# Pooling products in pairs between the gate projections, and five modulation units loaded into the work area

## The reference, cut to what matters

```python
h, gate_res = ada_modulate(x, c, norm_g, ada_w, ada_b)     # norm, scale and shift: silu(c) @ ada_w + ada_b
a, u, v, gate = split(h @ in_w)                            # four slices of 1024, 1024, 1024 and 2048 columns
ya = pool_mixer(a, pool_w, pool_scale)                     # windowed means, then 4 products of 256 x 256
yb = spatial_gating(u, v, sgu_norm_g, sgu_w, sgu_b)
y = concatenate([ya, yb]) * silu(gate)
x = x + gate_res * (y @ out_w)                             # 2048 x 1024
```

## Time and profile before

| What | us |
|---|---|
| median of three runs | 939.27 |
| the profiled execution, its own time | 939.58 |
| its span, first to last instruction | 937.8 |
| PE busy | 916.1 |
| DVE busy | 646.7 |
| ACT busy | 508.9 |

### The profile page before, as it was taken

How to read it: one execution, slowest core, us unless ns; L and a number is a source line. 1 busy time by engine, 2 the same in 40 slices (tenths; PEclk the granted TensorE clock), 3 DMA queues, 4 the chain that set the end, 5 groups by cost and what they waited for, 6 DMA issues and landing times.

```text
span 937.8 us, 19578 instructions
## 1 busy us (share of the span) xinstructions
PE 916.1 (98%) x8685; PEld 891.4 (95%) x8685; DVE 646.7 (69%) x754; ACT 508.9 (54%) x604; POOL 2.1 (0%) x14
## 2 busy tenths in 40 slices
PE   7999999999999999999999999999999999999998
PEld 6899999999999999999899999899889999999997
DVE  2897988785577467767689886557777665465565
ACT  3445445445554567963475654376646653455445
POOL 0000000000000000000000000000000000000000
PEclk9999999999999999999999999999999999999998
DMA  9999547974667544467444452234444556556521
GB/s 338 364 363 355 181 139 229 299 228 144 191 211 229 178 135 136 135 206 243 142 136 151 137 166 92 87 95 135 148 137 155 178 182 225 180 181 211 170 91 46
DMA packets 153440, 172.31 MB, mean 184 GB/s; under 512 B 4000, under 2 KB 137692, under 8 KB 153228
## 3 DMA queue, kind: packets, MB, share of 16 engines
q1 hardware_dynamic: 151696, 167.43, 55.2%
q10 hardware_dynamic: 1660, 3.63, 1.1%
HBM read 170.00 MB, written 1.05 MB: 182 GB/s over the span
## 4 chain that ended last, share of the span: by engine, by line
PE 79%; DVE 10%; ACT 5%; issue 3%; DMA 2%; ACTq 1%; DVEq 0%
PE pj L2695 64%; DVE w_lo L1502 2%; DMA work<-in_x_dram 1%; PE pj L2651 1%; ACT w_hi L1002 1%; PE pj L2653 1%; PE pj L2652 1%; PE pj L2480 1%; PE m_all L2387 1%; PE m_all L2370 1%; ACTq L965 1%; DMA rows<-in_ple_post_norm_dram 1%; PE m_all L2119 1%; DVE work L1935 0%; DVE work L2091 0%
## 5 line engine op out<-in xcount | busy, mean ns | idle before, releaser
L1502 DVE TENSOR_TENSOR w_lo<-raw,w_hi 128x2048 fp32r<-128x2048 f32 (+1 forms) x126 | 285.1, 2268 | 133.3 <-ACT w_hi L1002 132.6
L2695 PE MATMUL pj<-h_hi,w_hi 128*128 128x256 f32 (+1 forms) x1176 | 333.4, 284 | 2.3 <-issue 1.0
L2695 PE MATMUL pj<-h_lo,w_hi 128*128 128x256 f32 (+1 forms) x1176 | 328.3, 279 | 0.0
L2695 PE MATMUL pj<-h_hi,w_lo 128*128 128x256 f32 (+1 forms) x1176 | 328.1, 279 | 0.0
L1002 ACT ACTIVATE w_hi<-raw 128x2048 fp32r<-128x2048 f32 (+1 forms) x126 | 237.8, 1891 | 52.1 <-PE pj L2695 25.8
L2695 PEld LDWEIGHTS pj<-h_hi,w_hi 128*128 128x128 f32 (+1 forms) x1176 | 219.9, 187 | 6.0 <-issue 3.8
L2695 PEld LDWEIGHTS pj<-h_lo,w_hi 128*128 128x128 f32 (+1 forms) x1176 | 220.0, 187 | 0.4
L2695 PEld LDWEIGHTS pj<-h_hi,w_lo 128*128 128x128 f32 (+1 forms) x1176 | 219.9, 187 | 0.2
L2695 PE MATMUL pj<-y_lo,w_hi 128*128 128x256 f32 x624 | 174.2, 279 | 0.0
L2695 PE MATMUL pj<-y_hi,w_hi 128*128 128x256 f32 x592 | 165.7, 280 | 2.2 <-issue 2.2
L2695 PE MATMUL pj<-y_hi,w_lo 128*128 128x256 f32 x592 | 165.1, 279 | 0.0
(11 more groups left out here) (417 smaller groups left out, 1129.2 us busy)
## 6 DMA issues: line engine op xcount, KB each, us to landing
raw<-in_odd_in_w_dram SPq DMA_DIRECT2D x28, 1024.0 KB, 5.2
raw<-in_w_in_dram SPq DMA_DIRECT2D x23, 1024.0 KB, 5.3
raw<-in_ada_w_dram SPq DMA_DIRECT2D x22, 1024.0 KB, 7.4
raw<-in_w_ff_in_dram SPq DMA_DIRECT2D x16, 1024.0 KB, 5.4
raw<-in_w_ff_out_dram SPq DMA_DIRECT2D x16, 1024.0 KB, 5.1
raw<-in_even_in_w_dram SPq DMA_DIRECT2D x13, 1024.0 KB, 5.2
raw<-in_even_out_w_dram SPq DMA_DIRECT2D x8, 1024.0 KB, 6.1
raw<-in_odd_out_w_dram SPq DMA_DIRECT2D x8, 1024.0 KB, 5.1
```

The lines of the kernel that those rows point to most:

```text
L1502: V.tensor_tensor(lo[:, 0:n], raw_of(u)[:, 0:n], hi[:, 0:n].bitcast(F32), ALU.subtract).then_inc(done, 1)
L2695: m = nc.tensor.matmul(to, a_, b_, start=(s == 0 and q == 0 and (fb == 0 or not together)), stop=(s == len(steps_) - 1 and q == 2), skip_g ...
```

## The change

Four things change. The pooling jobs 0 and 1 stay before `ega` 0, but 2 and 3 now stand between `ega` 0 and `ega` 1. The modulation units that stand behind `ega` jobs stand behind 0 and 2, where it was 1 and 3. Five modulation units (15 to 19, now with the unit numbers 33, 36, 40, 43 and 46) no longer use the ring: they land in the work area, at places 0 and 35 in turn, once what lies there has been used. SP waits for that before it issues them.

```diff
-EARLY = {3: 8, 4: 16, 5: 24, 9: 116, 11: 124, 15: 116, 17: 124, 19: 116, 21: 124}
-REUSED = {9: 3, 11: 4, 15: 9, 17: 11, 19: 15, 21: 17}
+EARLY = {3: 8, 4: 16, 5: 24, 9: 116, 11: 124, 15: 116, 17: 124, 19: 116, 21: 124, 33: 0, 36: 35, 40: 0, 43: 35, 46: 0}
+REUSED = {9: 3, 11: 4, 15: 9, 17: 11, 19: 15, 21: 17, 33: 19, 36: 21, 40: 33, 43: 36, 46: 40}
-ADA_BEHIND = {"ev": (1, 2, 3), "ea": (0, 1, 2, 3), "ega": (1, 3)}
+ADA_BEHIND = {"ev": (1, 2, 3), "ea": (0, 1, 2, 3), "ega": (0, 2)}
...
-    def even(name, kind, w, c0, layout_="F"):
+    def even(name, kind, w, c0, layout_="F", before={}):
 
         for i in range(4):
+            for g in before.get(i, ()):
+                pool(g)
             job(name, kind, i, layout_, ...)
...
-    for g in range(4):
+
+    def pool(g):
         job("pool", "pool", g, "F", [pool_u], 2, 8 + 2 * g, lambda xc: ("p_lo", 1), k0=2 * g)
         jobs["pool", g]["late"] = True
-    even("ega", "gate", even_w, 3072)
+
+    even("ega", "gate", even_w, 3072, before={0: (0, 1), 1: (2, 3)})
...
                     if units[REUSED[u]]["ada"] is None:
                         split_done(sp, units[REUSED[u]])
+                    else:
+                        sp.wait_ge(S("ada_acc"), ADA_DVE.index(units[REUSED[u]]["ada"][2]) + 1)
+                if u == 33:
+                    sp.wait_ge(S("sgu_z"), 4)
+                if u == 36:
+                    sp.wait_ge(S("y_f"), 4)
```

## The result

The changed kernel takes 941.36 us (median of 9 runs, 940.16 to 942.57), the kernel before 938.19 us on the same chip (9 runs, 937.61 to 939.63). The ratio is 1.003, 95% interval 1.002 to 1.004: slower by about 3.2 us. The forecast was 941.8 us on a base of 939.27; as a difference it was +2.5 us. That 941.8 lies only 0.4 us from the measured time is partly luck: the base was 1.1 us higher than in this timing, and the difference 0.7 us too small.

A forecast was written before the change was run, and what follows sets the result against it. PE was taken as the bound, busy 916.1 of 937.8 us. Terms 0.53 + 2.1 + 0.3 less 0.33 gave +2.5 us, 942.1 on the profiled 939.58; less 0.3 to the median, 941.8 us, range 939.2 to 943.6.

The forecast's parts named there:

- Before `ega` 0: PE, with two pooling jobs less in front, waits for DVE's split: gap 1.55 us instead of 1.02, loss 0.53.
- Before `ega` 3: PE waits for DVE's late split of `ega` 3, which had been 2 us early: `ega` 3 starts 2.1 us late.
- Both named causes: Before `ega` 3: ACT's wait for the pooling jobs, and unit 16 and pooling copies, 4.7 us of DVE, before the split.
- Before `eo` 1: PE waits for DVE's split of `eo` 1: gap 1.4 us instead of 1.06, start 2.85 us later than before.
- signs named in advance: Expected in the changed kernel's profile: listed PE and ACT gaps, no long load waits, clock at 1.00, `eo` 3 ending 2.5 us later.
- Before `eo` 2: Unit 18 is loaded early from the freed buffers, so ACT's load wait and PE's 0.33 us gap go.
- The sum: At the end of `eo` 3: 0.53 + 2.1 + 0.3 less 0.33, given as +2.5 us.
- The waits of SP at nothing: SP's new waits before issuing units 33 and 36 cost 0; the nearest load margin is 13 us, bound +3.6.
- the freed ring counts: Rival: splits were late because of buffers, so all three PE gaps close: -2.41 us, 936.9; chance 0.06.
- ACT's wait does not bite: Rival: `ega` 2's upper half split runs right behind the one before, `ega` 3 on time: -0.9 us, 938.4; chance 0.12.
- The clock rival: Rival: the granted clock falls in a new PE gap, 1.7 us of work lost, 943.5; chance 0.08.

The follow-up runs named there:

- e1: Kernel before with only the pooling order changed (2 and 3 behind `ega` 0), modulation units as before: +1.3 us, ratio 1.0004 to 1.0021.
- e5: Changed kernel with the split of `ega` 2 done one slot later, ahead of the results of `ega` 1: -0.7 us against the kernel before.
- e4: Changed kernel with modulation units 15 and 16 back behind `ega` 1 and 3: +0.6 us against the kernel before.
- e3: Changed kernel with all four pooling products back in front of `ega` 0: -0.9 us against the kernel before.
- second profile: Changed kernel run again as the same program, with only an empty line added: +2.6 us against the kernel before, ratio 1.0028.
- e2: Kernel before with only the five modulation units landing in the work area, order unchanged: +0.2 us, ratio 0.9988 to 1.0007.
- e6: Kernel before with three pooling products in front of `ega` 0 and the last behind it: -0.1 us, ratio 0.9995 to 1.0013.
- e7: Kernel before with five modulation units in the work area, units 17 and 18 behind `eo` 1, 19 behind `eo` 2: -1.3 us.
- e8: Kernel before with the changes of e6 and e7 together: -1.7 us, ratio 0.9973 to 0.9991.

## Why the prediction was right, point by point

**Before `ega` 0.** Predicted a gap of 1.55 us instead of 1.02; measured 1.58, and 1.54 to 1.58 in every kernel with two pooling jobs in front. Right, shown by e1 and e5.

**Before `ega` 3.** Predicted 2.1; measured 2.07 and 2.17. Both named causes are shown: e5 takes away what queues behind ACT's wait, e4 takes unit 16 from in front, and either closes this gap; so does e3, which takes away the wait itself. The steps on the way also fit: ACT's half split predicted at 148.4, seen at 148.32 in a trace that runs 0.3 us ahead in this stretch.

**Before `eo` 1.** Predicted 1.4 in place of 1.06. The second profile has 1.33. The first has none, since the fallen clock had made PE late by itself: it cost 0.46 x 3.41 = 1.6 us of work and nearly all of it fell into this wait. The stretches differ by 0.1 us. So two of the signs named in advance, the gap of 1.2 us before `eo` 1 and the clock at 1.00 throughout the stretch, are missing in the first profile and came in the second; all the others are in both.

**Before `eo` 2.** Predicted that 0.33 us go: they did, in e2 as well, and in e1, where the units stay in the ring, they are still there. But e6 keeps the ring and has no such gap either: there ACT's wait for that load was 2.87 us instead of 3.59, and DVE's split was done at 186.8, before PE came at 187.35. So the gap hangs on the load, as predicted, but the freed ring is not needed to lose it.

**The sum.** Predicted +2.5, from the start of `eo` 1 (2.85 - 0.33); the four terms as written, 0.53 + 2.1 + 0.3 - 0.33, make 2.6, by rounding. The stretch says +2.7 and +2.6 (84.83 and 84.72 against 82.14), two timings say 3.2 and 2.6.

**The waits of SP at nothing.** e3 and e5 bear it out: they have the same two waits and are no slower than the kernel before. (In e2 the order is another and these waits are only 2.2 and 0.2 us, so e2 can't tell.) In the changed kernel SP waited 8.4 us for the fourth `sgu_z` product and 6.4 us for the gate product, and ACT waited for no load behind them. SP's list of waits there from 80 to 220 us, against the earlier trace rows:

```profile
SPq L929 <- DVE w_lo L1512: 103.6, 21, 10.3
SPq L914 <- PE m_all L2191: 8.4, 1, 8.4
SPq L916 <- DVE work L2101: 6.4, 1, 6.4
SPq L929 <- DVE cst_phase L1486: 3.8, 1, 3.8
```

**The rivals.** That the freed ring counts fell with e2. That ACT's wait does not bite fell with the profile: ACT was idle 4.44 us. Its price, though, was good: e5 was to come to -0.8 and came to -0.7 by the medians, -0.5 by the stretch. The clock rival was right in that the clock can fall in the new gap, and wrong in its price: I added 1.7 us without asking what lies behind. A loss in front of a race that another engine decides is hidden there up to the length of that race's wait.

**Where sums failed.** e1 and e4 were each put too high, by 0.4 and 0.8 us (by 0.7 and 0.8 in the stretches, near the 0.67 of the sums), through one place: I took the order of PE from the changed kernel where the partition sums had moved.

What stays open: whether the clock has a share in the time of the changed kernel, as the first timing lay 0.5 us above the stretch's difference. That is within its interval (1.9 to 3.8 us).

## What to carry to other kernels

Follow each in-order queue past the instruction that waits: a split done ahead of its need can hold back the result that the other engine lives on, and one line that puts the result first (e5) was worth about 3 us, where freeing buffers alone was worth nothing that could be told. Count a change race by race, at each place where one engine takes over from another, and carry the lateness on: what is won or lost before a race that another engine decides vanishes in it (e6, and the fallen clock), so the last race has to be won first (e6 alone gained nothing, e7 alone did). Compare the pace of the engine as well as its gaps before two stretches are set against each other. When a job is moved between others, redo the order on every engine for each variant, down to the small sums.

## What the runs showed of the hardware

The granted clock fell to half behind a gap of 2.07 us in one execution (0.54 on average from 161.44 to 164.85 us) and stayed at 1.00 behind one of 2.17 us in another of the same program. The same was seen from 590 to 596 us: 0.72 in the kernel before, 1.00 in the changed kernel's first profile, 0.76 in its second. So where the clock falls differs from run to run of the same work, and one profile with or without such a fall says nothing about a change. Time and mean clock go together in the timings: of the 33 runs of the kernel before beside e1 to e4, the nine with a mean granted clock of 0.999 or 1.000 have a median of 937.54 us, the nine at 0.996 or less 939.23. In the first timing of the changed kernel it is 940.68 (three runs at 1.000) against 941.9 (four at 0.996).

With the granted clock at 1.00, matmuls of 256 columns start 0.1167 or 0.1178 us apart for tens of microseconds at a time (10.50 and 10.60 us for 90 of them, in e7 and e8). What decides between the two no run shows.
